# Weighing the rows of v: low parts on VectorE, first loads issued a stage earlier

## The reference

```python
u = peer_u[ix]
a = jax.nn.gelu(jnp.einsum('td,thkd->thk', hx, u), approximate=False)
vsel = peer_v[ix]
return jnp.einsum('thk,thkd->td', gx * a, vsel)
```

## Time and profile before

| | us |
|---|---|
| median of 3 runs | 3216.41 (3214.94 to 3219.93) |
| the profiled execution | 3210.99 |
| its span | 3209.1 |
| PE busy | 2681.9 (84%) |
| DVE, ACT, POOL busy | 1333.8, 832.8, 973.8 |

### The profile page before, as it was taken

The page is one execution under the profiler, slowest core; times in us unless marked ns, Lnnn a source line. Parts: engine busy times, 40 slices in busy tenths (PEclk is TensorE's granted clock), DMA queues, the critical chain, the costliest instruction groups (busy, mean ns, idle before and its releaser), DMA issues. The chain is left out here.

```text
span 3209.1 us, 34563 instructions
## 1 busy us (share of the span) xinstructions
PE 2681.9 (84%) x12781; PEld 1868.0 (58%) x12781; DVE 1333.8 (42%) x2308; ACT 832.8 (26%) x1402; POOL 973.8 (30%) x485
## 2 busy tenths in 40 slices
PE   5985687999999986999999599765788888888886
PEld 2853577998999985787777466454222222222222
DVE  4346535995877765655556424432000000000001
ACT  2224222333666652333333322321000000000001
POOL 0030002666877766878887020000000000000000
PEclk8977798999999998999999799876999999999999
DMA  5332132455899998999998231025999999999996
GB/s 217 117 144 101 63 105 81 161 170 184 301 355 359 332 363 310 339 336 342 338 342 309 92 99 66 17 94 198 421 421 421 421 421 421 421 421 421 421 421 275
DMA packets 273859, 870.00 MB, mean 271 GB/s; under 512 B 30927, under 2 KB 124751, under 8 KB 221128
## 3 DMA queue, kind: packets, MB, share of 16 engines
q1 hardware_dynamic: 217136, 703.72, 57.7%
q0 software_dynamic: 38016, 138.43, 11.4%
q10 hardware_dynamic: 18584, 26.23, 2.2%
HBM read 812.69 MB, written 55.61 MB: 271 GB/s over the span
## 5 line engine op out<-in xcount | busy, mean ns | idle before, releaser
L562 PE MATMUL dots_dot_ps<-one_acts,dots_u_split 128*128 128x384 f32 x3072 | 555.8, 338 | 22.4 <-POOL dots_u_split L87 21.9
L689 PE MATMUL val_banks<-val_v,val_coef_split 128*128 128x512 f32 x2304 | 531.5, 391 | 42.0 <-DVE val_coef_split L87 41.9
L562 PEld LDWEIGHTS dots_dot_ps<-one_acts,dots_u_split 128*128 128x128 f32 x3072 | 533.6, 189 | 30.3 <-issue 21.9
L689 PEld LDWEIGHTS val_banks<-val_v,val_coef_split 128*128 128x128 f32 x2304 | 431.4, 188 | 142.0 <-issue 53.1
L87 POOL TENSOR_TENSOR dots_u_split<-dots_u_raw,dots_u_split 128x1024 fp32r<-128x1024 f32 x128 | 332.2, 2596 | 415.2 <-ACT dots_u_split L82 414.2
L87 POOL TENSOR_TENSOR val_v<-val_v_raw,val_v 128x2048 fp32r<-128x2048 f32 x64 | 297.8, 4654 | 84.0 <-ACT val_v L82 84.0
L960 PE MATMUL moe_up_ps<-all_raw_first,all_xs_t 128*64 128x512 f32 x1152 | 262.6, 597 | 57.7 <-DMA all_raw_first<-in_w_up 33.1
L1027 DVE TENSOR_TENSOR all_x<-moe_y_ps,all_x 128x512 f32<-128x512 f32 x64 | 44.3, 692 | 567.3 <-PE moe_y_ps L933 567.3
L653 DVE SCALAR_TENSOR_TENSOR val_banks<-val_v_rows,one_slot_coef,val_banks 128x1024 f32<-128x1024 f32 x128 | 164.5, 1285 | 218.3 <-DMA val_v_rows<-in_peer_v,one_expert 218.2
L960 PE MATMUL moe_up_ps<-moe_raw_more,all_xs_t 128*64 128x512 f32 x896 | 204.6, 597 | 50.6 <-DMA moe_raw_more<-in_w_up 42.5
L960 PEld LDWEIGHTS moe_up_ps<-all_raw_first,all_xs_t 128*64 128x64 f32 x1152 | 91.2, 136 | 226.7 <-issue 226.7
(11 more groups left out here) (329 smaller groups left out, 3186.2 us busy)
## 6 DMA issues: line engine op xcount, KB each, us to landing
all_raw_first<-in_w_gate SPq DMA_DIRECT2D x80, 1024.0 KB, 23.6
moe_raw_more<-in_w_down SPq DMA_DIRECT2D x80, 1024.0 KB, 24.2
dots_u_raw<-in_u_tiles SPq DMA_DIRECT2D x128, 512.0 KB, 4.1
val_v_raw<-in_peer_v SPq DMA_DIRECT2D x64, 1024.0 KB, 5.0
all_raw_first<-in_w_up SPq DMA_DIRECT2D x64, 1024.0 KB, 25.0
moe_raw_more<-in_w_up SPq DMA_DIRECT2D x64, 1024.0 KB, 25.3
moe_raw_more<-in_w_gate SPq DMA_DIRECT2D x48, 1024.0 KB, 23.6
all_raw_first<-in_w_down SPq DMA_DIRECT2D x48, 1024.0 KB, 25.3
```

Of the source, the lines that this page charges most:

```text
L562: last = self.nc.tensor.matmul(self.banks[:, j, 0:DENSE], self.split[:, j, u_part, k], self.h_t[:, h_part, k, T - DENSE:T], start=(k == 0 ...
L689: last = nc.tensor.matmul(banks[:, 2 * (t + 1) + half, :], coef_split[:, b, c_part, a, t * P:(t + 1) * P], v[:, b, v_part, a, half * BANK: ...
```

## The change

- The low part of v goes from POOL to DVE. POOL only gathers in the second stage.
- DVE's order in a turn becomes: low part of v, low part of the coefficients, the coefficients of the next turn, and two slots (of the turn before, so turn 0 has none and four stand at the end). The coefficients of turn 0 are computed ahead of the loop.
- Buffers for raw v, dots, gates and coefficients no longer have tiles of their own: they lie in `shared` (class `ValueRows`), whose contents are dead by then. Gates are read for two turns at once (768 KB, in pieces of 1 KB instead of 512 bytes).
- The loads of turns 0 and 1 (v and dots) are issued by SP in the first stage, ahead of the last six stores of gates, once half 0 of the staging area is stored; the gates of turns 0 and 1 are issued there too, once all gates are stored.
- In the first stage the slots are spread over 67 tiles instead of 72.
- SP's loop in the second stage is written out, with constants in its waits.

```diff
@@ peer_value_phase, SP
-                def load(turn, b, i):
-                    sp.wait_ge(v_lo, turn + 1)
-                    sp.dma_start(v_raw[:, b], ...).then_inc(v_loaded[b], 16)
-                    sp.wait_ge(coef_ready, turn * 2 + 2)
-                    sp.dma_start(dot[:, b], ...).then_inc(c_loaded[b], 16)
-                    sp.dma_start(weight[:, b]..., ...).then_inc(c_loaded[b], 16)
+                for turn in range(2, n_turns):
+                    sp.wait_ge(v_lo, turn - 1)
+                    values.load_rows(sp, turn)
+                    sp.wait_ge(coef_ready, 2 * (turn - 1))
+                    if turn % 2 == 0:
+                        values.load_weights(sp, turn // 2, weight_dram)
+                    values.load_dots(sp, turn, dots_dram)
@@ peer_value_phase, POOL
-                for c in range(sparse.NR):
+                for c in range(P):
                     sparse.gather(pool, c)
-                for turn in range(n_turns):
-                    b = turn % 2
-                    pool.wait_ge(v_hi, turn + 1)
-                    split_lo(nc.gpsimd, v[:, b, 1], v_raw[:, b], v[:, b, 0]).then_inc(v_lo, 1)
-                    for c in range(2 * turn + sparse.NR - 2, 2 * turn + sparse.NR):
-                        if sparse.NR <= c < P:
-                            sparse.gather(pool, c)
@@ peer_value_phase, DVE
+                coefficients(0)
+                for turn in range(n_turns):
+                    b = turn % 2
+                    dve.wait_ge(v_hi, turn + 1)
+                    split_lo(nc.vector, v[:, b, 1], v_raw[:, b], v[:, b, 0]).then_inc(v_lo, 1)
                     dve.wait_ge(coef_hi, turn + 1)
                     split_lo(nc.vector, coef_split[:, b, 1], coef[:, b], coef_split[:, b, 0]).then_inc(coef_lo, 1)
-                    add_slot(2 * turn + 1)
+                    if turn + 1 < n_turns:
+                        coefficients(turn + 1)
+                    if turn >= 1:
+                        add_slot(2 * turn - 2)
+                        add_slot(2 * turn - 1)
+                add_slot(P - 2)
+                add_slot(P - 1)
@@ peer_first_phase
-            return range(P * r // LEFT, P * (r + 1) // LEFT)
+            return range(min(P, P * r // (LEFT - 5)), min(P, P * (r + 1) // (LEFT - 5)))
@@ peer_first_phase, SP, behind the loads of u
+                sp.wait_ge(stored[0], 16 * PARTS * (SPANS // 2))
+                for turn in range(2):
+                    values.load_rows(sp, turn)
+                    values.load_dots(sp, turn, dots.dots_dram)
                 while part < PARTS * SPANS:
                     store_part(part // PARTS, part % PARTS)
                     part += 1
                 for b in range(2):
                     sp.wait_ge(stored[b], 16 * PARTS * (SPANS // 2))
+                values.load_weights(sp, 0, weight_dram)
+                for b in range(2):
                     sp.wait_ge(dots.stored[b], 16 + 16 * ETILES // 2)
@@ class ValueRows (new; its tiles are parts of shared)
+        self.raw = room(4 * D).rearrange("p (b a d) -> p b a d", b=2, a=2)
+        self.dot = room(4 * DENSE).rearrange("p (b a t) -> p b a t", b=2, a=2)
+        self.coef = room(4 * DENSE).rearrange("p (b a t) -> p b a t", b=2, a=2)
+        self.weight = room(8 * DENSE).rearrange("p (b s a t) -> p b s a t", b=2, s=SPANS, a=4)
+    def load_weights(self, sp, pair, weight_dram):
+        sp.dma_start(self.weight[:, pair % 2]...,
+                     weight_dram[:, :, 4 * pair:4 * pair + 4, :]...).then_inc(self.weight_loaded[pair % 2], 16)
```

More of the change, by code:

```diff
@@ L573, in activate, with peer_value_phase @@
                       self.gelu[:, j]).then_inc(self.stored[j], 16)
-def peer_value_phase(nc, A, dots_dram, weight_dram, x, gate, expert, slot_coef, gathered):
+def peer_value_phase(nc, A, dots_dram, weight_dram, x, gate, expert, slot_coef, gathered, values):
     DT = DENSE // P
     with Scope(nc, "val") as s:
-        v_raw = s.sb("v_raw", [P, 2, 2, D])
+        v_raw, dot, weight, coef, part = values.raw, values.dot, values.weight, values.coef, values.part
         v = s.sb("v", [P, 2, 2, 2, D], F32R)
-        dot = s.sb("dot", [P, 2, 2, DENSE])
-        weight = s.sb("weight", [P, 2, SPANS, 2, SPAN])
-        coef = s.sb("coef", [P, 2, 2, DENSE])
         coef_split = s.sb("coef_split", [P, 2, 2, 2, DENSE], F32R)
-        part = s.sb("part", [P, 2, BANK])
         sparse = SparseTokens(nc, s, A["peer_v"], expert, "v", gathered)
@@ L590, in peer_value_phase @@
         sparse_sum = banks[:, 0:2, :].rearrange("p a n -> p (a n)")
-        v_loaded = [s.sem(f"v_loaded{i}") for i in range(2)]
-        c_loaded = [s.sem(f"c_loaded{i}") for i in range(2)]
+        v_loaded, dot_loaded, weight_loaded = values.v_loaded, values.dot_loaded, values.weight_loaded
         v_hi, v_lo, coef_ready, coef_hi, coef_lo, summed, dve_step, zeroed = (s.sem(x_) for x_ in (
@@ L623, in split @@
                     split_hi(nc.scalar, v[:, b, 0], v_raw[:, b]).then_inc(v_hi, 1)
-                    act.wait_ge(coef_ready, turn * 2 + 6)
+                    act.wait_ge(coef_ready, turn * 2 + 2)
                     split_hi(nc.scalar, coef_split[:, b, 0], coef[:, b]).then_inc(coef_hi, 1)
@@ L655, in add_slot, with coefficients @@
                         in1=sparse_sum, op0=ALU.mult, op1=ALU.add).then_inc(sparse.used, 1)
[L657 to L660, removed]
+                def coefficients(turn):
+                    b, pair = turn % 2, turn // 2
+                    dve.wait_ge(dot_loaded[b], 16 * (turn // 2 + 1))
+                    dve.wait_ge(weight_loaded[pair % 2], 16 * (pair // 2 + 1))
+                    if turn >= 2:
+                        dve.wait_ge(coef_lo, turn - 1)
                     for a in range(2):
@@ L664, in _ @@
                             dot[:, b, a].rearrange("p (s t) -> p s t", s=SPANS),
[L665 to L666 removed]
+                            weight[:, pair % 2, :, 2 * (turn % 2) + a, :], ALU.mult).then_inc(coef_ready, 1)
+                coefficients(0)
[3 more added lines that the diff above has]
+                    split_lo(nc.vector, v[:, b, 1], v_raw[:, b], v[:, b, 0]).then_inc(v_lo, 1)
                     dve.wait_ge(coef_hi, turn + 1)
                     split_lo(nc.vector, coef_split[:, b, 1], coef[:, b], coef_split[:, b, 0]).then_inc(coef_lo, 1)
[L669 removed]
+                    if turn + 1 < n_turns:
[5 more added lines that the diff above has]
+                add_slot(P - 1)
                 step = Steps(dve, dve_step)
@@ L682, in multiply @@
                 def multiply(turn, b, first=False, final=False):
-                    pe.wait_ge(v_lo, turn + 3)
-                    pe.wait_ge(coef_lo, turn + 3)
+                    pe.wait_ge(v_lo, turn + 1)
+                    pe.wait_ge(coef_lo, turn + 1)
                     for a in range(2):
@@ L1085, in wait, with peer_first_phase @@
         eng.wait_ge(self.gathered[c % self.NR], 16 * (c // self.NR + 1))
-def peer_first_phase(nc, A, ident, dots, shared, score, choice, h_row, expert, slot_coef, weight_dram, gathered):
+def peer_first_phase(nc, A, ident, dots, shared, score, choice, h_row, expert, slot_coef, weight_dram, gathered, values):
     CHOICE, LAG, SET = 28, 4, 8
@@ L2093, in _, with __init__, room, load_rows @@
                         y_seq(nc.vector.tensor_tensor(hy_y[:, c, :], hy_y[:, c, :], short[:, 2 + c, :], ALU.mult))
+class ValueRows:
+    def __init__(self, nc, s, A, shared):
+        self.A = A
+        at = 0
+        def room(n):
+            nonlocal at
+            at += n
+            return shared[:, at - n:at]
+        self.raw = room(4 * D).rearrange("p (b a d) -> p b a d", b=2, a=2)
+        self.dot = room(4 * DENSE).rearrange("p (b a t) -> p b a t", b=2, a=2)
+        self.coef = room(4 * DENSE).rearrange("p (b a t) -> p b a t", b=2, a=2)
+        self.weight = room(8 * DENSE).rearrange("p (b s a t) -> p b s a t", b=2, s=SPANS, a=4)
+        self.part = room(2 * BANK).rearrange("p (o n) -> p o n", o=2)
+        self.v_loaded, self.dot_loaded, self.weight_loaded = (
+            [s.sem(f"{n}_loaded{i}") for i in range(2)] for n in ("v", "dot", "weight"))
+    def load_rows(self, sp, turn):
+        sp.dma_start(self.raw[:, turn % 2], self.A["peer_v"][turn * (2 * P):(turn + 1) * (2 * P), :].rearrange(
+            "(a e) d -> e a d", e=P)).then_inc(self.v_loaded[turn % 2], 16)
+    def load_dots(self, sp, turn, dots_dram):
+        sp.dma_start(self.dot[:, turn % 2], dots_dram[2 * turn:2 * turn + 2].rearrange(
+            "a e t -> e a t")).then_inc(self.dot_loaded[turn % 2], 16)
+    def load_weights(self, sp, pair, weight_dram):
+        sp.dma_start(self.weight[:, pair % 2].rearrange("p s a t -> p s (a t)"),
+                     weight_dram[:, :, 4 * pair:4 * pair + 4, :].rearrange(
+                         "s b a t -> b s (a t)")).then_inc(self.weight_loaded[pair % 2], 16)
 def program(nc, A, out, taps=None):
```

16 lines of the change are left out of this document (3 added, 13 removed).

## The result

| | before | after |
|---|---|---|
| median of 20 runs, us | 3215.64 | 3221.16 |
| ratio, after to before | | 1.0022, 95% interval 1.0012 to 1.0032 |
| profiled execution, us | 3210.99 | 3227.56 |

The change makes the kernel slower by about 0.2%, 5.5 us by the medians, where 25 us of gain were forecast. That is little, but clear of the noise: the whole interval lies above 1. The two profiled executions lie on opposite sides of their medians, so their difference (16.6 us) is larger; the parts that follow come from them and carry a scatter of some 2 to 3 us each.

A forecast was written before the change was run, and what follows sets the result against it. PE was taken to bound the second stage, with a small leak, plus a border pause. Gains of 13.4 us in the steady turns and 11.5 at the border, rounded to 25, gave 3191 us from a median of 3216.41; range 3182 to 3207.

The forecast's parts named there:

- What bounds the kernel before: Second stage: PE is the bound, 8.26 us a turn when nothing is late, with a small leak from DVE's order and late gathers.
- the leak of 14.4 us: Second stage: PE's waits for the coefficients' low part on DVE, of which the forecast left 1 us.
- the whole 17.3: Second stage: PE's time above 528.6 us for 64 turns: 14.4 of waits, 2.0 of lower clock, 0.9 of small gaps.
- DVE's list: Steady turns after the change: DVE's work adds to 6.89 us a turn, under PE's 8.26, with 1.37 us left over.
- That is tight in every second turn, but the 3.0 and 1.37 us take it: Steady turns: gates' loads take 8 us and a landing, issued some 9 us before use; PE-path slack 3.0, DVE's spare 1.37.
- 13.4 us of gain: Steady turns: 14.4 us of PE's waits fall to 1; bounds of the gain 15.3 and 0.
- The border: Between the stages: stores end at 1205.5, PE starts at 1214.5 instead of 1225.97; gain 11.5 us, bounds 16 and 5.
- the missing gathers make way for the early loads: Border: 3.31 MB of gathers go away and 2.8 MB of loads come, so the stores end at 1204 to 1207.
- rival 2: Border gives almost nothing: the loads push the stores back by their full 6.7 us; net gain 18.5, 3198 us; chance 0.08.
- The first stage: Slots over 67 tiles: 67 KB of transfer and 0.16 us of DVE more a tile, costed at nothing, covered by PE's work.
- Rival 4: Nothing gained in the steady turns: PE's waits stay because v or gates come late; gain 11.5, 3205 us; chance 0.06.
- Rival 3: DVE becomes the bound: late gathered rows make the turn 10.3 us; 3318 us; slower from about 1.8 us a turn; chance 0.06.

The follow-up runs named there:

- experiment 1: The changed kernel with SP issuing a turn's gates and dots ahead of its raw v, not behind it: 3182.1 us, 0.9886 of before.
- experiment 6: The changed kernel with gates and dots ahead of v in the turns, and the four early loads behind the six last stores: 3180.97 us, 0.9897.
- experiment 9: As experiment 6, but turn 1's early loads of v and dots go behind the first gates: 3174.83 us, 0.9875.
- experiment 7: The changed kernel with the gates of a pair loaded in the odd turn before, behind its dots; v still ahead of dots: 3187.98 us, 0.9927.
- experiment 10: The changed kernel with each pair's gates loaded a second time, between the gates and the dots in SP's list: 3321.94 us, 1.0338.
- experiment 11: The changed kernel with each pair's gates loaded a second time, behind the dots in SP's list: 3213.29 us, 0.9996.
- Experiment 2: The changed kernel with the four early loads of v and dots issued behind the last six stores of gates: 3219.27 us, 1.0007.
- experiment 3: The changed kernel with the slots of the first stage spread over 72 tiles again: 3229.41 us, 1.0036.
- experiment 5: The kernel of experiment 1 with the low part of v back on POOL, between the gathers: 3260.63 us, 1.014.
- experiment 8: The kernel before, with both slots of a turn behind the low part of the coefficients on DVE: 3242.95 us, 1.0087.

## Why the prediction was wrong

- **What bounds the kernel before: right.** PE at 8.2 us a turn is the floor, and the leak of 14.4 us was there to be had: experiments 1, 6 and 9 reach it. Their second stage is 21 us shorter, more than the whole 17.3, as PE's turn is 8.20 and not 8.26.
- **DVE's list: right.** The low part of v took 2.28 us (2.35 forecast, bounds 2.32 and 2.45: just under the lower one), the rest as priced. Gathers with two turns of lead ceased to be late.
- **"That is tight in every second turn, but the 3.0 and 1.37 us take it": the step that failed.** The transfer was sized well ("8 us and a landing"; 9.8 to 12.6 measured, 10.8 in the mean), its lead less so ("some 9 us before use"; DVE stood ready after 6.5). What was wrong is that a slack was set against the difference. The issue of the loads hangs on DVE's low part of v, which stands behind the wait for the last loads. That is a loop over two turns: 10.0 of landing, 1.0 for SP, 1.0, 2.6 and 2.2 on DVE are 16.8 us in the round shown, 17.6 in the mean, where PE needs 16.4. Slack absorbs a delay that comes once; a loop returns it every time. Not 13.4 us of gain but 21.1 of loss in the trace. The rounds of the changed kernel and experiments 1, 7, 10 and 11 show it.
- **The clock in the turns: not forecast, and of little weight.** Pauses of 2 to 3 us were followed by spells at the lower clock, 8.5 us in PE's account, but in a stage that DVE's loop paced.
- **The border: sign right, size off.** 11.5 us of gain forecast, 7.4 measured in the pause. The step that failed is that the missing gathers make way for the early loads: the stores should have ended 7.0 us behind PE's last product of u, and ended 11.2 behind it, at 1214.1. From there to PE's start 8.9 us passed, 9.0 forecast. Experiment 2 gives the stores 8.7 us back, so rival 2 had the mechanism right, and the trace agrees with the rule cited beside this term from the Trainium skill, "DMA: Bandwidth & Descriptors", section "Queues, rings and completion order". With the order of experiment 9 the pause is 13.4, under the 16 forecast.
- **The first stage: right**, nothing, by experiment 3.
- **Rivals.** Rival 4 named the wait, "v or gates come late instead", but priced it as no gain; it had no bound above, and the measured 3221 lies beyond its 3205 and beyond the range. Rival 3 had the form of the mechanism, a wait in DVE's list that makes DVE the bound, with the wrong transfer. Its threshold held: "slower than before from a wait of about 1.8 us a turn on", where the dots cost DVE 4.3 us every second turn, 2.2 a turn. Neither got the chance it deserved.

## What to carry to other kernels

Where a load's issue waits for an engine that itself waits for the last load, add up the round: issue, landing, and everything that stands between the two waits on that engine. If the sum is longer than the busiest engine needs for the turns that the loop spans, the loop sets the pace, and no slack elsewhere helps. And on an in-order queue, issue each load on the release of its own buffer: one early wait for another buffer takes the lead from all that stand behind it.

## What was not expected of the hardware

- A DVE instruction with two SBUF inputs waits out a POOL subtraction in SBUF: two products, 1.03 us together, took 5.94 with a POOL instruction of 4.59 us inside, in nearly every turn of experiment 5. DVE's slots, with one input in PSUM, kept 1.28 to 1.29 us. The Trainium skill, "SBUF — State Buffer", section "Who interferes with whom", has the rule; the prediction used it for one row only. The expectation of experiment 8 weighed it for the low part of the coefficients alone, and the mere reordering cost 28 us through the products.
- POOL's issue of a gather took 2.74 us when it began inside DVE's low part of v (at 1401.32 and 1407.91 in the changed kernel), and 0.94 otherwise; on average 1.80 against 1.10 before, and 0.97 in experiment 1, where the low part starts behind the gathers. It cost nothing here: DVE did not wait for a gathered row in the steady turns of either.
- The granted clock fell to 0.50, the 1.2 GHz level, for a few us behind some pauses of PE of 2 to 3 us in an otherwise full stage (540.0 against 531.5 us for the same products); behind others, as the one of 2.41 us ahead of 1333.12, it did not.
